# A hybrid transformer kernel on one core: GpSimd's low part of the next weight tile moves ahead of its sine product

## What is computed

```python
for i in range(4):
    kind = i % 3                                   # A, B, C, A
    h = rms_norm(x, norm_g[i]) * (1.0 + sc) + sh   # hc likewise, for the context
    u, z = split(h @ w_in)                         # u = q, k, v of all heads
    # every kind: q, k = rms_norm(q), rms_norm(k)
    # A and C:    q, k = axial_rope(q), axial_rope(k)
    o = attention(q, [kc, k], [vc, v])             # C: softmax pair 0 - lam * pair 1
    x = x + gt * ((o * silu(z)) @ w_out)           # context too, but for the last layer

def _rotate(x, ang):
    x1, x2 = split(x)
    return concatenate([x1 * cos - x2 * sin, x2 * cos + x1 * sin])
```

## Time and profile before

| | |
|---|---|
| runs | 2413.1, 2417.28 and 2423.98 us, median 2417.28 |
| profiled execution | 2411.85 us, its span 2410.1 us |
| mean granted TensorE clock | 0.942 |
| TensorE busy | 2201.5 us (91%) |
| VectorE busy | 1258.7 us (52%) |
| ScalarE busy | 1049.5 us (44%) |
| GpSimd busy | 927.4 us (38%) |
| low parts on GpSimd (line 295) | 262, 630.6 us, 2409 ns each |
| mean DMA | 109 GB/s |

### The profile page before, as it was taken

The page is one execution under the profiler, slowest core; times in us unless marked ns, Lnnn a source line. Parts: engine busy times, 40 slices in busy tenths (PEclk is TensorE's granted clock), DMA queues, the critical chain, the costliest instruction groups (busy, mean ns, idle before and its releaser), DMA issues.

```text
span 2410.1 us, 39591 instructions
## 1 busy us (share of the span) xinstructions
PE 2201.5 (91%) x14736; PEld 1843.7 (77%) x14736; DVE 1258.7 (52%) x2646; ACT 1049.5 (44%) x2009; POOL 927.4 (38%) x598
## 2 busy tenths in 40 slices
PE   5899899988998998989999989999999799788998
PEld 4798799978988996767777966777697466567777
DVE  5854467477445663356653054565216577624553
ACT  4353565445436645433334253333325355534333
POOL 0565386027456810323332122332214344422443
PEclk8899899999999998999999998998999899889998
DMA  6343666644356665211124312112322211222111
GB/s 234 114 148 108 191 179 185 198 155 133 117 163 188 194 189 183 73 71 36 36 71 140 97 53 88 53 62 71 103 72 88 70 36 36 79 78 97 62 62 53
DMA packets 72849, 262.93 MB, mean 109 GB/s; under 512 B 8032, under 2 KB 10208, under 8 KB 72416
## 3 DMA queue, kind: packets, MB, share of 16 engines
q1 hardware_dynamic: 71392, 256.31, 33.5%
q0 software_dynamic: 1280, 4.20, 0.6%
HBM read 259.43 MB, written 1.05 MB: 108 GB/s over the span
## 4 chain that ended last, share of the span: by engine, by line
PE 71%; DVE 13%; ACT 6%; issue 5%; POOL 4%; DMA 1%; DVEq 0%; ACTq 0%; SPq 0%; POOLq 0%
PE gemm L437 15%; PE gemm L438 14%; PE gemm L439 14%; PE gemm L713 7%; PE score L752 5%; PE obank L784 4%; PE tbank L673 3%; POOL w_lo L295 2%; DVE d L1405 1%; PE obank L788 1%; PE stat L680 1%; DVE zt L1367 1%; DVE zh L1366 1%; PE gemm L643 1%; PE obank L522 1%
## 5 line engine op out<-in xcount | busy, mean ns | idle before, releaser
L295 POOL TENSOR_TENSOR w_lo<-ring,w_hi 128x1024 fp32r<-128x1024 f32 x262 | 630.6, 2409 | 641.0 <-ACT w_hi L949 639.4
L437 PE MATMUL gemm<-g_hi,w_hi 128*128 128x256 f32 x1344 | 391.4, 291 | 32.6 <-DVE w_lo L295 10.7
L437 PE MATMUL gemm<-h_hi,w_hi 128*128 128x512 f32 (+1 forms) x928 | 396.3, 427 | 13.1 <-POOL w_lo L295 13.1
L949 ACT ACTIVATE w_hi<-ring 128x1024 fp32r<-128x1024 f32 x344 | 360.9, 1052 | 104.8 <-PE gemm L439 36.5
L438 PE MATMUL gemm<-g_lo,w_hi 128*128 128x256 f32 x1344 | 380.6, 283 | 0.0
L439 PE MATMUL gemm<-g_hi,w_lo 128*128 128x256 f32 x1344 | 380.2, 283 | 0.0
L438 PE MATMUL gemm<-h_lo,w_hi 128*128 128x512 f32 (+1 forms) x928 | 355.4, 383 | 0.0
L439 PE MATMUL gemm<-h_hi,w_lo 128*128 128x512 f32 (+1 forms) x928 | 354.6, 382 | 0.0
L437 PEld LDWEIGHTS gemm<-g_hi,w_hi 128*128 128x128 f32 x1344 | 260.9, 194 | 51.4 <-issue 24.3
L437 PEld LDWEIGHTS gemm<-h_hi,w_hi 128*128 128x128 f32 x928 | 181.7, 196 | 149.8 <-issue 105.2
L1274 ACT ACTIVATE pr<-score,small 128x512 f32<-128x512 f32 (+1 forms) x192 | 127.9, 668 | 372.9 <-DVE small L1689 370.7
(11 more groups left out here) (293 smaller groups left out, 3812.9 us busy)
## 6 DMA issues: line engine op xcount, KB each, us to landing
ring<-wall SPq DMA_DIRECT2D x478, 512.0 KB, 3.7
r<-nbias POOLq DMA_DIRECT2D x16, 256.0 KB, 3.0
cst<-consts SPq DMA_DIRECT2D x1, 2340.5 KB, 10.2
r<-x_t SPq DMA_DIRECT2D x1, 1024.0 KB, 5.0
x<-ctx_t SPq DMA_DIRECT2D x1, 1024.0 KB, 15.4
y_t<-x SPq DMA_DIRECT2D x4, 256.0 KB, 2.3
d<-pos SPq DMA_DIRECT2D x1, 128.0 KB, 10.1
```

The lines of the kernel that those rows point to most:

```text
L295: eng.tensor_tensor(w_lo[:, q % SPLITS, :, :], ring[:, t % RING, :, :], w_hi[:, q % SPLITS, :, :].bitcast(F), ALU.subtract)\
L437: pe.matmul(out, w[0][:, k, :], x[0], start=start, stop=False)
L949: act.activation(w_hi[:, q % SPLITS, :, :], ring[:, t % RING, :, :], ACT.Copy).then_inc(S["hi_ready"], 1)
```

## The change

In `q_side` the two steps of GpSimd change places: the low part of the tile now comes before the sine product.

```diff
                 def q_side(c):
+                    split_to(qz_tile(2 * c + 1))
                     if kind != "B":
                         sin_mul(rbase(L) + nk + c, NQ, cc("sinx", 0, NQ))
-                    split_to(qz_tile(2 * c + 1))
```

## The result

| | before | new |
|---|---|---|
| median of four runs | 2420.11 us (2413.1 to 2423.98) | 2391.43 us (2387.05 to 2392.69) |
| profiled execution | 2411.85 us, span 2410.1 | 2391.46 us, span 2389.7 |
| mean granted TensorE clock | 0.942 | 0.945 |

The new kernel is 28.7 us faster: ratio 0.9882, interval 0.9853 to 0.991. The forecast was a gain of 14.3 us and a range down to 2393 us, so about half of the gain came from somewhere the sum did not look.

A forecast was written before the change was run, and what follows sets the result against it. TensorE, busy 91% of the span, was taken as the bound. First A 3.0 plus C 11.3 gave 14.3 us: 2411.85 to 2397.5 us profiled, 2403 us against the 2417.28 us median; 8-in-10 range 2393 to 2418 us.

The forecast's parts named there:

- addition without company: Line 1405's query addition on VectorE, no longer beside GpSimd's low part, takes 0.69 instead of 2.70 us.
- The first A: TensorE's 0.5 us wait for the query addition goes at six columns: 3.0 us gained.
- The slot: The tile's ring slot comes free some 4 to 8 us earlier, with SyncE's refill; nothing waits for it.
- the new wait at `to_keys`: In C, TensorE waits about 1.15 us for VectorE's `combine`, in place of the old 1.32 us wait.
- C, the clock: In C, TensorE's clock stays up after the new wait; columns gain 1.75 us, and up to 10.2 us is lost otherwise.
- the first rival: Clock stays down in C after the new wait: a column wins only 0.17 us, total 2412 us; chance 0.20.
- the row of 2.26 us: Profile stretch with 2.26 us of TensorE work, followed by clock 1.00; taken as nearest, so C's clock holds.
- The 2.51 us row: Profile stretch with 2.51 us of TensorE work, followed by clock 0.50; cited for the clock staying down in C.
- The last A: First query: another VectorE step held 2.16 us more, addition freed of 2.1 us, net 0; later columns also 0.
- a sum without the shared port: At the last A's first query, without a shared SBUF port, moving the step would cost and win nothing.

The follow-up runs named there:

- The experiment with query 1 alone: Against before, the low part goes ahead of the sine product only at query 1 in all layers of kinds A and C: 2396.97 us, ratio 0.9904.
- one product more, once: New kernel with one score product of C made twice (column 2, unit 1), meant to shift later columns: 2390.98 us, ratio 0.989 to before.
- all queries but query 1: New order (low part ahead of the sine product) at every query except query 1, which keeps the old order: 2403.33 us, ratio 0.994 to before.

## Why the prediction was half right

*The addition* (its "addition without company"): right. 0.69 us or less in all 16 additions of 128x512.

*The first A*: right for what it was about. 0.53 us went from each of the five later distances, for 0.5 forecast. The first two distances gave 11.4 us instead of 0.5.

*The slot*: this is the step that failed. The prediction put it at nothing: "The tile's slot comes free some 4 to 8 us earlier, and SyncE's refill with it; nothing here waits for that." The amount holds for the columns whose rows it rested on, and was carried over to all. In column 0 of the first A the low part comes earlier by much more (18.8 us, by the gate product), and TensorE waited there for just this refill. The change had been costed from a middle column. The rows of 5.76 and 7.38 us stood in the trace of before; it takes TensorE's waits for transfers and SyncE's own waits over the whole layer to see them. The experiment with query 1 alone puts 21.5 us on this place, 18.8 us of it in the first two distances of the first A and of C in its trace.

*C, the new wait at `to_keys`*: right in kind and size, 1.15 us forecast, 1.12 and 0.99 us measured (0.29 us in column 7). In the column shown TensorE was ready 6.95 us after its first scores and started 7.94 us after them; the forecast had 6.7 and 7.8. One link differs: VectorE's first maximum now waits for TensorE's scores (3.44 us), not for the power.

*C, the clock*: wrong for most columns. The one distance that half clock did not lengthen (2 to 3) gained 2.05 us, forecast 1.75. In the others the gain was 0.12 to 0.51 us, and the first rival had said 0.17. C's five later distances gave 3.0 us, where five times 1.75 would be 8.8. The choice of the row of 2.26 us as the nearest was the right reading of the stretch with the wait, which indeed was not followed by 0.50; but another stretch of the column, which had not been asked about, was. The 2.51 us row ("with tiny products of line 732 in it") was the hint. Nor is the pattern fixed: the kernel with the last A's query in the old order is the same program through C, and there its distances were 24.08, 25.27, 25.64, 27.20, 27.57 and 26.86 us.

*The last A*: right. In its first query the low part held VectorE's other step for 2.12 us, forecast 2.16, and the addition came down to 0.42 us. TensorE's wait for it was 6.13 us, as before:

```profile
2203.87 2.81 DVE L1366 SCALAR_TENSOR_TENSOR zh<-zh,zs 128x512 f32<-128x512 f32 x1
...
2210.06 0.42 DVE L1405 TENSOR_TENSOR d<-d,rot 128x256 f32<-128x256 f32 x1 [0.53 <-POOL rot L1872]
```

The stall had only moved. The later columns stayed at 17.22 us. Here the rule of the Trainium skill, page "SBUF — State Buffer", section "Who interferes with whom", holds, within a tenth of a microsecond of the forecast; a sum without the shared port would have had 0.69 us for line 1366.

So two errors of opposite sign: some 6 us too much in C's later columns, and about 20 us missing at the slot. The last is what carried the time out of the range.

*What stays open.* What brings half clock to C's later columns. Counting its stretches in columns 2 to 7, one trace of each kernel: with the wait at `to_keys` there were 5 (new kernel), 5 (one product more, once), 4 (last A's query 0 old) and 1 (all queries but query 1); with that wait taken away or filled there were 1, 1, 1 and 0. So the wait seems to be a part of what brings it, and it is not sufficient. The stretch that precedes half clock is another one, some 14 us ahead of the wait's, and two kernels that are the same program through C gave 5 and 4, so chance or the place of the columns has a share that no run measured. The two versions that would have asked more of the slot, a fifth slot in the ring and a low part behind the power at every query, were not run.

## What to carry to other kernels

Before moving a step that consumes a tile from a shared ring, look at the waits of the queue that refills the ring, over all columns and not only a middle one: a wait of 20 us there for the moved engine says that its place in the order may set when the data of a later product arrives. On an engine that works in order, put steps that release something ahead of steps that wait for something late. Cost the edges of a loop apart from its middle; here three boundaries at the edges were worth more than all the others.

## What the runs showed of the hardware that I had not expected

A step of VectorE as small as a `tensor_scalar` of 128x2 took 1.71 us beside GpSimd's low part, and 0.23 us once that stood behind it. Two reciprocals of 128x2 just ahead of it, beside the same low part, took 0.15 and 0.17 us. I had thought only of steps with two large inputs.

The granted clock fell to 0.50 behind a stretch that was 3.16 of 3.42 us busy, and stayed at 1.00 behind one with 2.43 us. The busy share of the stretch ahead did not tell which would come. With a redundant product in TensorE's wait of 1.0 us, five columns were 6.2 us shorter in sum than with the wait left (one trace of each; the same program through C as the new kernel's differed from it by 1.5 us there).
